# Gram products that open the recurrence, rotation by accumulating transfers, low-rank products apart, and residual adds ahead of weight splits, in a two-layer hybrid decoder trunk

## The reference

```python
for l in range(2):
    h = rms_norm(x, mix_norm[l])
    p = h @ w_in[l]                            # 1024 x 3200 or so, columns split in three groups
    y_rwkv = rwkv7_mix(token_shift(p_rwkv))    # 6 heads of 64
    y_conv = short_conv_mix(p_conv)
    y_attn = dilated_attention_mix(p_attn)     # 6 heads of 64, q and k normed and rotated
    x = x + concat(y_rwkv, y_conv, y_attn) @ w_o[l]
    h = rms_norm(x, ffn_norm[l])
    x = x + (swiglu(h) if l == 0 else moe_swiglu(h))   # dense 3584, then top 2 of 8 experts

def rope(x):                                   # on q and k
    return concatenate([x1 * cos - x2 * sin, x2 * cos + x1 * sin])

def step(state, r, w, k, v, a, b):             # the recurrence of rwkv7_mix, a = -kk, b = kk * gate
    sa = einsum('hvk,hk->hv', state, a)
    state = state * w + outer(sa, b) + outer(v, k)
    return state, einsum('hvk,hk->hv', state, r)

v = v + (v_first - v) * sigmoid(v0 + pv @ v2)  # layer 1 alone; w, a and g come from such low-rank products too
```

## Time and profile before

| What | us |
|---|---|
| median of 3 executions | 1598.84 |
| lowest and highest | 1595.59 and 1601.77 |
| the profiled execution | 1595.95 |
| its span | 1594.1 |
| PE busy | 1562.1 (98%) |
| DVE busy | 1269.2 (80%) |
| ACT busy | 1072.2 (67%) |
| POOL busy | 68.2 (4%) |

### The profile page before, as it was taken

One profiled execution on the slowest core, in us unless ns is written; L12 is line 12 of the kernel. 1 busy time (PEld: TensorE's weight loads), 2 busy tenths in 40 slices (PEclk: granted clock), 3 DMA queues, 4 the chain that ended last, 5 costly groups with the idle time before them and its releaser, 6 DMA issues.

```text
span 1594.1 us, 29162 instructions
## 1 busy us (share of the span) xinstructions
PE 1562.1 (98%) x11182; PEld 1364.9 (86%) x11182; DVE 1269.2 (80%) x1450; ACT 1072.2 (67%) x1321; POOL 68.2 (4%) x72
## 2 busy tenths in 40 slices
PE   8999999999999999999999999999999999999998
PEld 8978999999999788788888888888888888888886
DVE  5676655444556867899999999999999999999996
ACT  5445354444454455788888888888888888888885
POOL 0012000000000310000000100100100000000000
PEclk9999999999999999999999999999999999999999
DMA  8500555555444006999999999999999999999995
GB/s 311 212 2 4 185 196 180 182 184 184 148 133 158 3 3 250 336 382 372 376 395 369 380 395 365 382 394 366 374 395 370 384 392 366 381 394 366 385 380 163
DMA packets 189562, 446.28 MB, mean 280 GB/s; under 512 B 8080, under 2 KB 10656, under 8 KB 189344
## 3 DMA queue, kind: packets, MB, share of 16 engines
q1 hardware_dynamic: 186480, 434.52, 74.6%
q0 software_dynamic: 2304, 7.87, 2.1%
q10 hardware_dynamic: 688, 2.62, 0.5%
HBM read 438.69 MB, written 6.29 MB: 279 GB/s over the span
## 4 chain that ended last, share of the span: by engine, by line
PE 94%; DVE 3%; ACT 1%; issue 1%; DMA 0%; POOL 0%; SPq 0%; DVEq 0%; ACTq 0%; POOLq 0%
PE bank L768 27%; PE bank L770 27%; PE bank L769 27%; PE bank L749 9%; PE bank L1434 2%; ACT w_hi L1513 1%; DMA ring<-in_w_in 0%; PE bank L789 0%; DVE w_lo L2196 0%; PE bank L1397 0%; PE bank L1178 0%; PE bank L939 0%; DVE ring L2019 0%; DVE w_lo L1943 0%; PE bank L1069 0%
## 5 line engine op out<-in xcount | busy, mean ns | idle before, releaser
L1513 ACT ACTIVATE w_hi<-ring 128x1024 fp32r<-128x1024 f32 x812 | 858.4, 1061 | 330.4 <-PE bank L770 320.4
L2196 DVE TENSOR_TENSOR w_lo<-ring,w_hi 128x1024 fp32r<-128x1024 f32 x672 | 814.3, 1224 | 66.2 <-ACT w_hi L1513 16.5
L768 PE MATMUL bank<-w_hi,acts_hi 128*128 128x512 f32 (+1 forms) x1376 | 539.7, 392 | 3.5 <-DVE w_lo L2196 3.4
L770 PE MATMUL bank<-w_hi,acts_lo 128*128 128x512 f32 (+1 forms) x1376 | 533.6, 388 | 0.0
L769 PE MATMUL bank<-w_lo,acts_hi 128*128 128x512 f32 (+1 forms) x1376 | 533.0, 387 | 0.0
L768 PEld LDWEIGHTS bank<-w_hi,acts_hi 128*128 128x128 f32 x1376 | 258.9, 188 | 55.4 <-DVE w_lo L2196 4.5
L770 PEld LDWEIGHTS bank<-w_hi,acts_lo 128*128 128x128 f32 x1376 | 258.8, 188 | 53.9
L769 PEld LDWEIGHTS bank<-w_lo,acts_hi 128*128 128x128 f32 x1376 | 259.2, 188 | 50.7
L768 PE MATMUL bank<-acts_hi,w_hi 128*128 128x256 f32 x884 | 254.4, 288 | 3.4 <-DVE acts_lo L2103 1.7
L769 PE MATMUL bank<-acts_lo,w_hi 128*128 128x256 f32 x884 | 251.7, 285 | 0.0
L770 PE MATMUL bank<-acts_hi,w_lo 128*128 128x256 f32 x884 | 251.6, 285 | 0.0
(11 more groups left out here) (243 smaller groups left out, 1098.3 us busy)
## 6 DMA issues: line engine op xcount, KB each, us to landing
ring<-in_moe_wg SPq DMA_DIRECT2D x112, 1024.0 KB, 7.0
ring<-in_moe_wu SPq DMA_DIRECT2D x112, 1024.0 KB, 7.1
ring<-in_moe_wd SPq DMA_DIRECT2D x112, 1024.0 KB, 7.0
ring<-in_w_in SPq DMA_DIRECT2D x24, 1024.0 KB, 7.5
ring<-in_dense_wg SPq DMA_DIRECT2D x14, 1024.0 KB, 5.3
ring<-in_dense_wu SPq DMA_DIRECT2D x14, 1024.0 KB, 5.1
ring<-in_dense_wd SPq DMA_DIRECT2D x14, 1024.0 KB, 4.9
ring<-in_w_o SPq DMA_DIRECT2D x8, 1024.0 KB, 5.2
```

Source lines behind the costliest of these rows:

```text
L768: pe.matmul(out_, a_hi, b_hi, start=first, stop=False, **kw)
L770: return pe.matmul(out_, a_lo, b_hi, start=False, stop=final, **kw)
L1513: return act.activation(o, i, ACT.Copy, **kw)
L2196: TT(w_lo[:, q, :], raw, w_hi[:, q, :].bitcast(F32), ALU.subtract).then_inc(lo_ready, 1)
```

## The change

Eight edits, of which the diff has the core.

1. `rot` and `turn_heads` are gone. The sign of the rotation is in the sine table. DVE multiplies q and k by sine into `sq_qk` and by cosine in place, two instructions from SBUF, and POOL issues four accumulating transfers of 32 x 1536 in each layer, which add the swapped halves onto q and k. `scores(l, 0)` waits for them; `lora_wa` no longer waits for the rotation.
2. The low-rank products g stand behind piece 2 of chunk 0, v behind piece 3.
3. Chunk 1 waits for its pieces one by one.
4. `scores(l, 0)` moves ahead of the last tile of chunk 3. The transposes of v and k move out from ahead of the Gram products into levels 1 to 4, one `token_major` in each, through bank 0.
5. The Gram products are regrouped: b and k are multiplied with a and r in one product of 64 x 128 columns (`with_a_and_r`), for one parity of heads at a time. There are 84 products in place of 132, 48 of them wide. Two of the wide groups of the odd heads stand inside level 1. POOL masks three matrices instead of two, DVE two halves instead of four.
6. DVE splits two pieces of `w_o` behind levels 1 and 2 instead of around the Gram matrices. ACT loads the table of the exponential earlier.
7. Behind the output projection DVE adds first and splits the first piece of the next weights behind add 0 and the second behind add 2 (before: ahead of add 0 and behind it).
8. Two `keep_awake` products are gone in the norm behind the mixers of layer 0, and two in the one ahead of layer 1.

```diff
@@ gpsimd
+            def add_swapped(l):
+                pool.wait_ge(rope_ready, l + 1)
+                for r0 in range(0, P, HD):
+                    for a, b in ((r0, r0 + HD // 2), (r0 + HD // 2, r0)):
+                        pool.dma_start(pT[a:a + HD // 2, 16:22, :], sq_qk[b:b + HD // 2, :, :],
+                                       accum_op=ALU.add).then_inc(swapped_in, 16)
             for l in range(L):
+                add_swapped(l)
                 pool.wait_ge(unit_done, SINGLE0[l] + SINGLE[l])
...
@@ tensor, project
-                if first and ch in SPLIT_IN:
-                    pe.wait_ge(lo_ready, IN0[l, ch] + 4)
...
+                    if first and ch in SPLIT_IN and k % 2 == 0:
+                        pe.wait_ge(lo_ready, IN0[l, ch] + k // 2 + 1)
@@ tensor, recurrence
+                def with_a_and_r(x, b, h, c):
+                    q, e = c % 2 * C, h % 2 * HD
+                    o = bank[b + c // 2][q:q + C, 0:2 * NRT * C].rearrange("p (s i t) -> p s i t", s=2, i=NRT)
+                    return mm(o[:, :, h // 2, :], feature_block(x, h, c), a_and_r[e:e + HD, :, h // 2, c * C:(c + 1) * C])
...
-                gram_product(bT, aT, 4, True).then_inc(gram_done, 1)
-                gram_product(aT, bT, 6, True).then_inc(gram_done, 1)
-                gram_product(bT, aT, 0, False, (1,)).then_inc(gram_done, 1)
+                for (h, c), (h2, c2) in zip(pairs_of((0,)), pairs_of((1,))):
+                    with_a_and_r(bT, 4, h, c)
+                    last = narrow(bT, aT, 1, h2, c2)
+                last.then_inc(gram_done, 1)
+                for h, c in pairs_of((0, 1)):
+                    last = narrow(aT, bT, 6 + h % 2, h, c)
+                last.then_inc(gram_done, 1)
                 pe.wait_ge(sc_read, HEADS * l + 1)
-                gram_product(kT, aT, 2).then_inc(gram_done, 1)
+                for h, c in pairs_of((0,)):
+                    last = with_a_and_r(kT, 2, h, c)
+                last.then_inc(gram_done, 1)
...
+                    if lev < 5:
+                        token_major((vT, kT)[lev // 3], (lev - 1) % 2, 0)
                     turn_probs(l, lev - 1)
@@ tensor, hooks
-                HOOKS = {2: {1: lambda: head_spread(2 * l, 6, (5, 6, 7)), 3: turn_heads}, 0: {1: lora_wa, 3: lora_gv}}
+                HOOKS = {2: {1: lambda: head_spread(2 * l, 6, (5, 6, 7))}, 0: {1: lora_wa, 2: lora_g, 3: lora_v}}
...
-                    keep_awake(2, 2)
                     sum_squares(1, KT - 2)
...
-                        keep_awake(1, 2)
                         sum_squares(2, 6)
@@ vector, rotation
-                for i in range(3):
-                    TT(sq_qk[:, 2 * i:2 * i + 2, :], bank[5 + i][:, :].rearrange("p (i t) -> p i t", i=2),
-                       spread(const("sin"), 2), ALU.mult)
-                then(TT(qk, qk, spread(const("cos"), 6), ALU.mult))
-                TT(qk, qk, sq_qk, ALU.add).then_inc(rope_ready, 1)
+                TT(sq_qk, qk, spread(const("sin"), 6), ALU.mult)
+                TT(qk, qk, spread(const("cos"), 6), ALU.mult).then_inc(rope_ready, 1)
@@ vector, behind the recurrence
-                first_pieces(range(0, 1))
                 for j in range(4):
...
-                    if j == 0:
-                        first_pieces(range(1, 2))
+                    if j in (0, 2):
+                        first_pieces(range(j // 2, j // 2 + 1))
```

More of the change, by code:

```diff
@@ L192, in decoder_trunk @@
         ALL = 2 * QUAD
-        gram = [keep.take(ALL) for _ in range(4)]
+        grams = keep.take(4 * ALL)
+        gram = [grams[:, n * ALL:(n + 1) * ALL] for n in (0, 2, 1, 3)]
+        k_grams = grams[:, 2 * ALL:4 * ALL].rearrange("p (s e u x) -> p e u s x", s=2, e=2, u=2)
         inv_w, a_gate, tmp1, tmp2 = [g.rearrange("p (i t) -> p i t", i=NRT) for g in gram]
@@ L842, in project @@
                 ns = [halves[("in", l, ch, hf)] for hf in range(2)]
-                if first and ch in SPLIT_IN:
-                    pe.wait_ge(lo_ready, IN0[l, ch] + 4)
-                elif first:
+                if first and ch not in SPLIT_IN:
                     for m in ns:
@@ L1221, in _, with lora_wa @@
                 us = units(l)
-                def turn_heads():
+                def lora_wa():
                     pe.wait_ge(hs_used, 2 * l + 1)
-                    for i in range(6):
-                        last = mm(bank[5 + i // 2][:, i % 2 * T:i % 2 * T + T], const("rot"), pT[:, 16 + i, :])
-                    last.then_inc(rot_done, 1)
-                def lora_wa():
-                    pe.wait_ge(rope_ready, l + 1)
                     pe.wait_ge(lora_act, l + 1)
@@ L1625, in keep_tok, with keep_b, keep_k, keep_lt @@
                     copy(o, bank[b][:, 0:RW]).then_inc(tok_kept, 1)
[L1627 to L1635 removed]
+                def keep_b(e, b):
+                    if e:
+                        act.wait_ge(gram_done, 5 * l + 4)
+                    else:
+                        act.wait_ge(invt_ready, 12 * l + 1)
+                    copy(half(gram[2], e).rearrange("p (u x) -> p u x", u=2), two_banks(b, 1)).then_inc(b_kept, 1)
+                def keep_k(n, e):
+                    act.wait_ge(gram_done, 5 * l + n)
+                    copy(k_grams[:, e], psum[:, 2:4, 0:2 * NRT * C].rearrange("p u (s x) -> p u s x", s=2)).then_inc(
+                        k_kept, 1)
+                def keep_lt(lev, e):
+                    act.wait_ge(lt_done, 10 * l + 2 * (lev - 1) + e + 1)
+                    copy(half(lt, e), bank[e][:, 0:QUAD]).then_inc(lt_kept, 1)
                 exponentials(l, 0)
[L1637 removed]
+                keep_k(3, 0)
                 for lev in range(1, 6):
@@ L1640, in recurrence @@
                         keep_probs(l, lev - 2)
-                    for e in range(2):
-                        act.wait_ge(lt_done, 10 * l + 2 * (lev - 1) + e + 1)
-                        copy(half(lt, e), bank[e][:, 0:QUAD]).then_inc(lt_kept, 1)
+                    keep_lt(lev, 0)
                     if lev == 1:
-                        keep_raw(1, 2)
+                        keep_b(1, 2)
+                        keep_b(0, 4)
+                    keep_lt(lev, 1)
+                    if lev == 1:
+                        keep_k(5, 1)
                     else:
                         exponentials(l, lev - 1)
+                    if lev < 5:
+                        keep_tok(lev - 1, (tok_v, tok_k)[lev // 3][:, (lev - 1) % 2 * RW:((lev - 1) % 2 + 1) * RW], 0)
                     if lev == 5:
```

168 lines of the change are left out of this document (84 added, 84 removed).

## The result

The kernel after takes 1580.74 us (median of 4, 1580.36 to 1581.95) against 1599.44 for the kernel before: ratio 0.9887, interval 0.9872 to 0.9903. Two more sets on other chips gave 1581.71 against 1595.56 (0.9907, 0.9892 to 0.9923) and 1581.06 against 1597.78 (0.9890, 0.9869 to 0.9910). The kernel after repeats itself to 2.5 us; the kernel before spreads over 5 to 8 us and its median moves with the set, so the gain reads 18.7, 13.9 and 16.7 us. The two profiled executions, 1595.95 and 1580.65, are 15.3 apart.

The account below looks back on a forecast made before the run. PE was taken as the bound (busy 1562 of 1594 us), changeable only between 45 and 640 us. Terms 5.1 + 4.7 + 3.15 + 2.35 - 2.4 + 3.6 = 16.5 us, against median 1598.84, gave 1582; 8-in-10 range 1576 to 1591.

Parts of the forecast that it names:

- a: Rotation: six products leave PE's path in each layer, about 2.55 us each time, with the transfers hidden; gain 5.1 us.
- slower rival: Accumulating transfers come late and PE stops at the first scores; at twice the price 1632 us; chance 0.04.
- b: Low-rank products and chunk 1: g and v apart, clock drop gone in layer 1, shorter split wait in layer 0; gain 4.7.
- c: Start of the Gram products: they start sooner, 2.1 us in layer 0 and 1.05 in layer 1; gain 3.15.
- d: Gram products and level 1: PE's list takes 11.8 us; gain 1.9 and 0.45, together 2.35.
- rival 2: Wide Gram products don't pay: 230 ns each, 11 us lost in all, gain 5.5, time 1593; chance 0.06.
- e: Levels 2 to 4: three more transposes in each, 0.41 us, six times; a loss of 2.4 us.
- rival 4: Levels bound by DVE or ACT, 1 us for each of eight; gain 8, time 1591; chance 0.07.
- f: Norms: wait for squares, clock drop and keep_awake products go; 2.7 us at layer 0's root, 0.9 ahead of layer 1; gain 3.6.
- Rival 1: Clock drops and one gap come back, about 7 us lost; gain 9.5, time 1589; chance 0.20.

Follow-up runs that it names:

- awake_back: The kernel after with the two keep_awake products back in each of the two norms; 1581.11 us.
- transfers_late: The kernel after, but POOL issues the four accumulating transfers only when the tile before the last of the projection is done; 1602.81 us.
- lowrank_back: The kernel after with g and v again by turns behind piece 3 of chunk 0, and one wait for all pieces ahead of chunk 1; 1584.45 us.
- scores_back: The kernel after with each layer's first scores behind the projection's last tile and behind the waits of the Gram products; 1587.32 us, one execution.
- scores_behind: The kernel after with each layer's first scores behind the projection's last tile but ahead of the waits of the Gram products; 1580.86 us, one execution.
- recurrence_alone: The kernel before with only the recurrence changed (place of first scores, Gram products, transposes inside levels, w_o splits); 1592.53 us, ratio 0.9973.

## Why the prediction was right, point by point

The forecast was 1582 and 16.5 us of gain. The medians are 1580.7 to 1581.7, the traces 15.3 apart. Two misses met in the 1582: the sum was 1.2 too high, and the 2.9 us by which the median of before lay above its profiled execution were carried over whole, while the kernel after has 0.1 (1580.74 and 1580.65). So part of the closeness is luck. By the table:

- **a**, 5.1: 2.6 in layer 0. In layer 1 the lead grew by 1.85 from the root to the w and a products, with a new drop in that stretch. It takes 52.30 there in the kernel before, 50.45 in the kernel after and 49.53 in awake_back, which has no drop: so the rotation gave 2.8 and the drop took 0.9. The transfers were hidden, with more cover than needed. But my bound for them was off in both its parts: one takes 8.9 us, not at most 7.9, and they run side by side, so all four took under 10 us and not up to 32 (transfers_late). The row that I took it from goes to `out`, and beside it the page before has a second kind of accumulating transfer, `to_half` of 256 KB at 5.7. The slower rival would have needed them some 25 us later than they are.
- **b**, 4.7: 0.5 + 3.6 = 4.1. The bracket of the wait shrank by 0.66, as I had taken, but the landmarks give 0.5 of it (lowrank_back). The work was right, and the drop went, which was the uncertain half. lowrank_back shows that the order by turns brings a drop, but only 1.7 of the 3.4.
- **c**, 3.15: layer 0 gave 2.0 (2.52 less the 0.5 of b) for 2.1, layer 1 1.6 for 1.05. My sign for it, a start within 0.3 us of the end of `bT`, holds in layer 1 (0.1); in layer 0 PE is still at its last tile when `bT` ends, 1.5 us earlier. "It can't start sooner" was wrong: the last operand itself was 0.6 shorter. Since the scores stand ahead of the last tile, that tile ends later and POOL's copies, which wait for it, no longer run beside DVE's instruction: 0.95 instead of the 1.58 of the earlier trace rows. I had both rows and did not ask what the move of the scores does to POOL. scores_back and scores_behind bring the 1.58 back.

The Trainium skill (SBUF — State Buffer, Who interferes with whom) says that a VectorE instruction with two tensors as inputs, both in SBUF, contends with GpSimd's reads. 0.95 alone against 1.58 beside the copies agrees.

- **d**, 2.35: 2.0 + 0.6. The list of PE's groups, 11.8 us, came out as 11.70 in both layers. The unseen price, a wide product, was 105 ns for my 116, far from the 230 of rival 2. My bounds for it were miscounted: with 96 wide products 230 ns gives -8.6 and 58 ns gives 7.9, where I wrote -10 and 4.5. No drop came, and in recurrence_alone, with everything ahead as before, none came either.
- **e**, -2.4: -1.0 and -0.7. Three transposes cost 0.39, but the three that turn the probabilities are 0.06 cheaper behind them: a level takes 5.57 instead of 5.24. In layer 1 of the kernel before level 2 took 5.56 already, so only two levels grew there. No wait came in the levels: rival 4 had no part.
- **f**, 3.6: this is the step that was mis-sized. 2.7 at the first root was right to the tenth, but not in its parts. The order gave 1.2 (0.94 in my sum) and the two products nothing (0.45). The other 1.5 (1.3) are the drop ahead of the root, and it was not tied to the wait as I had it: of the three traces with the old order and its wait, one has it. Behind the roots two drops came. Between the roots the lead shrank by 0.6, with the 0.9 of two products in it, and the second drop took some 0.9 of what layer 1's rotation gave. So f brought about 1.2 net. awake_back shows the exchange: with the products back both drops are gone, and its trace is 1 to 1.5 us shorter; the medians can't tell. I had counted `keep_awake` as pure cost.

Rival 1 (drops come back) was thus true for one of three places, and its price was some 2.3 us, not 7. The sum came within 1.2 us of the two traces because f's miss of 2.4 was partly made up by a, c, d and e, each 0.2 to 0.7 above its term; that too is luck.

Not settled: why the drop behind the low-rank products of layer 1 is 3.4 us long with the rotation gone and 6.8 with it, and what brings the drops at 612 and at the first root in some executions.

## What to carry to other kernels

Follow the lead of one trace over the other from landmark to landmark: fifteen microseconds of a kernel of 1600 were found so to a few tenths at each place, where medians of the kernel before alone differ by 5. When a product that only keeps PE busy is taken out, look at the clock in the stretch behind it, not at its own duration: here two such products, 0.9 us at the second root and nothing at the first, went with full clock behind the root, and the drop without them cost about as much. Look also at more than one trace of the kernel before: the drop that I counted as its own at the first root is missing in one of two traces of that order with those products. And ask of each moved piece which other engine starts by its end; the copies of POOL that way lengthened or spared a DVE instruction on the critical path.

## What the runs showed of the hardware

- Accumulating transfers from SBUF to SBUF of 192 KB took 8.9 us (median) from issue to landing with the weights' transfers in flight, 6.1 without them in transfers_late; there four issued within 3.4 us were all in after 9.6.
- A wide product of 64 x 64 by 128 columns in plain fp32 takes 105 ns where one of 64 columns takes 58 with one parity of heads alone: twice the columns cost 1.8 times.
- Idling of 2.05 us ahead of the Gram products was followed by 13.5 us at half clock (scores_back), and of 8.9 us by about 6 us behind it (transfers_late), while 1.20 and 0.37 at the same place had none behind them; the 2.05 and the 1.20 are one execution each. Behind the roots, in dense work, a drop lasted some 3.5 us each time. In the Gram products, of small tiles, it lasted 13.5 us in scores_back, but some 3.5 in the kernel before.
- A drop of some 3.5 us takes 1.7 us of PE work, but behind the roots what follows came only 0.6 to 1.3 us later.
- An instruction of DVE with two inputs from SBUF and two copies of POOL, all of 128 x 768, took 2.56 us together where the three alone sum to 2.61 (scores_behind): they did not overlap to any gain.
- "issue" in a bracket can be a plain wait: in both scores kernels PE started 0.1 us after DVE's instruction ended.
